# Two steps of the down product moved ahead of a release, and two stores moved ahead of four loads

## What is computed

```python
h = _rmsnorm(x, attn_norm[l])
z = h @ w_in[l]                       # GLA heads and MLA heads
...
x = x + jnp.concatenate([o_gla, o_mla], axis=-1) @ w_out[l]
h = _rmsnorm(x, mlp_norm[l])
x = x + jnp.square(jax.nn.relu(h @ w_up[l])) @ w_down[l]
```

## Time and profile before

| | |
|---|---|
| median of 3 runs | 1158.79 us (1158.64 to 1160.03) |
| the profiled execution's own time | 1160.03 us |
| its span, first to last instruction | 1158.1 us |
| TensorE busy | 1126.1 us, 97% |
| VectorE, GpSimd, ScalarE busy | 786.6, 529.6, 468.7 us |
| mean granted TensorE clock | 0.997 of full speed |
| moved by transfers | 158.42 MB, 137 GB/s |

### The profile page before, as it was taken

The page is one execution under the profiler, slowest core; times in us unless marked ns, Lnnn a source line. Parts: engine busy times, 40 slices in busy tenths (PEclk is TensorE's granted clock), DMA queues, the critical chain, the costliest instruction groups (busy, mean ns, idle before and its releaser), DMA issues.

```text
span 1158.1 us, 15248 instructions
## 1 busy us (share of the span) xinstructions
PE 1126.1 (97%) x5582; PEld 899.3 (78%) x5582; DVE 786.6 (68%) x1092; ACT 468.7 (40%) x891; POOL 529.6 (46%) x429
## 2 busy tenths in 40 slices
PE   5999999999999999999999999999999999999998
PEld 5977677776766768887788888888887888888887
DVE  5575776637777772157488755775798888988863
ACT  5343544315565562056423223322434344344341
POOL 2352442514344363235844444444536565564562
PEclk9998999999999999999999999999999999999999
DMA  7332242372212114323334334331589784466642
GB/s 244 88 110 64 81 149 81 91 224 63 74 33 60 51 38 153 120 92 128 108 112 161 110 127 143 112 109 72 200 288 340 257 296 147 131 188 216 203 120 89
DMA packets 98346, 158.42 MB, mean 137 GB/s; under 512 B 9248, under 2 KB 38960, under 8 KB 98272
## 3 DMA queue, kind: packets, MB, share of 16 engines
q1 hardware_dynamic: 96720, 152.53, 40.0%
q10 hardware_dynamic: 1008, 3.67, 0.9%
q0 software_dynamic: 544, 1.24, 0.6%
HBM read 115.46 MB, written 41.94 MB: 136 GB/s over the span
## 4 chain that ended last, share of the span: by engine, by line
PE 83%; DVE 9%; issue 3%; POOL 2%; ACT 1%; DMA 1%; SPq 0%; ACTq 0%; DVEq 0%; POOLq 0%
PE ps L1808 78%; PE ps L2043 2%; PE ps L1880 1%; DVE g_cum L1375 1%; DVE t_all L1580 1%; DVE t_new L1580 1%; DVE dr_lo L1580 1%; POOL wi_lo L753 1%; DMA gain<-in_attn_norm_dram 1%; DMA up_raw<-in_w_up_dram 1%; PE ps L1823 0%; PE ps L1945 0%; DVE stage L1580 0%; DVE m_qk L1349 0%; DVE m_nm L1525 0%
## 5 line engine op out<-in xcount | busy, mean ns | idle before, releaser
L1808 PE MATMUL ps<-dr_hi,dl_hi 128*128 128x512 f32 x448 | 174.5, 390 | 1.6 <-DVE dr_lo L1580 1.6
L1808 PE MATMUL ps<-dr_hi,dl_lo 128*128 128x512 f32 x448 | 174.3, 389 | 0.0
L1808 PE MATMUL ps<-dr_lo,dl_hi 128*128 128x512 f32 x448 | 174.3, 389 | 0.0
L882 POOL TENSOR_TENSOR ua_lo<-up_raw,ua_hi 128x1024 fp32r<-128x1024 f32 x46 | 116.8, 2541 | 118.3 <-ACT ua_hi L918 118.3
L904 POOL TENSOR_TENSOR dl_lo<-l_raw,dl_hi 128x512 fp32r<-128x512 f32 x64 | 101.5, 1610 | 70.2 <-ACT dl_hi L918 69.8
L1808 PE MATMUL ps<-wi_hi,a_hi 128*128 128x512 f32 (+1 forms) x256 | 105.9, 414 | 5.3 <-POOL wi_lo L753 3.8
L1808 PE MATMUL ps<-a_hi,ua_hi 128*128 128x512 f32 x256 | 99.9, 390 | 2.0 <-ACT u_two L918 1.8
L904 POOL TENSOR_TENSOR dl_lo<-s_all,dl_hi 128x512 fp32r<-128x512 f32 x48 | 75.0, 1582 | 58.4 <-ACT dl_hi L918 57.7
L1808 PEld LDWEIGHTS ps<-dr_hi,dl_hi 128*128 128x128 f32 x448 | 84.1, 188 | 20.3 <-issue 2.8
L1808 PE MATMUL ps<-a_lo,ua_hi 128*128 128x512 f32 x256 | 99.6, 389 | 0.0
L1808 PE MATMUL ps<-a_hi,ua_lo 128*128 128x512 f32 x256 | 99.6, 389 | 0.0
(11 more groups left out here) (218 smaller groups left out, 2422.9 us busy)
## 6 DMA issues: line engine op xcount, KB each, us to landing
r_raw<-in_w_down_dram SPq DMA_DIRECT2D x144, 256.0 KB, 3.4
hidden<-stage SPq DMA_DIRECT2D x72, 256.0 KB, 2.1
up_raw<-in_w_up_dram SPq DMA_DIRECT2D x16, 1024.0 KB, 5.5
l_raw<-hidden SPq DMA_DIRECT2D x64, 256.0 KB, 3.3
raw<-in_w_in_dram SPq DMA_DIRECT2D x24, 256.0 KB, 3.0
z_gla<-z_stage SPq DMA_DIRECT2D x16, 256.0 KB, 2.0
raw<-in_w_out_dram SPq DMA_DIRECT2D x16, 256.0 KB, 6.7
xs<-in_x_dram SPq DMA_DIRECT2D x8, 512.0 KB, 7.2
```

Source lines behind the costliest of these rows:

```text
L882: pool.tensor_tensor(ua_lo[n % UP_RING][:, :, :], up_source(g, product), ua_hi[n % UP_RING][:, :, :].bitcast(F32), ALU.subtract).then_inc( ...
L1808: return pe.matmul(dst, lhsT, rhs, start=start, stop=stop, skip_group_check=onto)
```

## The change

In `up_group` for the last group, all four steps 0 to 3 of the down product are prepared ahead of the `u_three` additions; before, steps 0 and 1 were ahead of them and 2 and 3 behind. On SP, the stores of tiles 5 and 7 of the last group go ahead of loads 8 and 9, and the other three stores (8, 9, 6) ahead of loads 10 and 11; before, loads 8 to 11 were all issued ahead of these five stores. Nothing else changes.

```diff
--- before.py
+++ after.py
@@ -693,13 +693,13 @@
             sp.wait_ge(ulo_done, turn_of(UG - 1, P3) + 1)
             for t in range(2, 8):
                 down_load(t)
-            hidden_stores(UG - 1, (3, 4, 2))
-            for t in range(8, 12):
+            hidden_stores(UG - 1, (3, 4, 2, 5, 7))
+            for t in range(8, 10):
                 down_load(t)
-            hidden_stores(UG - 1, (5, 7, 8, 9, 6))
+            hidden_stores(UG - 1, (8, 9, 6))
 
             sp.wait_ge(ulo_done, UP_PRODUCTS)
-            for t in range(12, PAIRS):
+            for t in range(10, PAIRS):
                 down_load(t)
 
             sp.wait_ge(part_ready, 2 * UP_PRODUCTS)
@@ -1702,7 +1702,7 @@
                     dve.wait_ge(p1_out, 2 * g + i + 1)
                     tt(u, made(g, P6, i), u, ALU.add).then_inc(u2_ready, 1)
                 if g + 1 == UG:
-                    down_steps(0, 2)
+                    down_steps(0, 4)
                 for i in range(2):
                     dve.wait_ge(u2_ready, 2 * g + i + 1)
                     if g >= 1:
@@ -1710,8 +1710,6 @@
                     tt(u_three[:, i, :], made(g, P7, i), u_two[:, g % 2, i, :], ALU.add).then_inc(u3_ready, 1)
                 if g + 1 < UG:
                     up_sums_one(g + 1)
-                else:
-                    down_steps(2, 4)
                 if g == 0:
 
                     dve.wait_ge(x2_stored[NB // 2 - 1], 32)
```

## The result

| | before | after |
|---|---|---|
| median of 6 runs | 1158.86 us | 1169.18 us |
| lowest to highest | 1156.43 to 1160.54 | 1165.86 to 1170.42 |
| profiled execution, its span | 1160.03, 1158.1 | 1166.39, 1164.5 |
| mean granted clock of that execution | 0.997 | 0.996 |

The ratio is 1.0081, 95% interval 1.0064 to 1.0097: slower by 10.3 us or 0.9% on the medians, and above the range's 1167.5. The changed kernel run a second time gave 1168.52 against 1158.34 us, ratio 1.0091 (1.0076 to 1.0106). The forecast was 5.0 us.

A forecast was written before the change was run, and what follows sets the result against it. TensorE, busy 97% of the span, was taken as the bound, waiting 2.3 us for VectorE. Waits of 2.4 + 4.9 = 7.3 us against 2.3 add 5.0 to the median 1158.79: 1163.8 us, range 1160.2 to 1167.5.

The forecast's parts named there:

- Part 1: VectorE, steps 2 and 3 ahead of `u_three`: first `u_three` at 844.65, so P4 waits 2.4 us, bounds none to 4.3.
- Part 2, the issue: SP's queue: load 8 is issued at 861.9, 13 us later than before, behind stores 5 and 7 waiting for data.
- supply, 5.0 us: Loads 8 to 12 at 0.75 us per transfer make quad 2 wait: 5.0 us more TensorE waiting in all, chance 62%.
- low 11: End of `down_low(11)` on VectorE, which quad 2's fourth step needs: forecast 878.7 against 873.70 before.
- 0.6 + 0.6 us: VectorE's `down_sum(12)` and then `down_low(11)` after load 12's last transfer, 0.6 us each.
- upper bound of 8.0: Supply loss if each transfer takes 0.93 us: `down_low(11)` ends at 881.7, +8.0 us.
- 1.63 us of waiting between 870 and 874 at full clock: Trace evidence against a clock fall: TensorE with that waiting and 9 matmuls stayed at clock 1.00.
- the fall at 94 to 96 us: Trace evidence on the clock: granted clock goes from 1.00 to 0.50 where 4 matmuls start in 2 us.
- P4's wait alone counts: Rival: supply is quick enough, quad 2's fourth step only +0.1 us, 1158.9; 16% together with late supply under 2.3 us.
- The other side: Rival: early steps 2 and 3 at 0.6 us per operation remove quad 2's wait, giving back 2.3 us, 1156.5; chance 5%.
- The clock falls: Rival: TensorE's clock halves for some 6 us around 872 to 879, costing 3 us more, 1166.8; chance 15%.
- The catching up of steps 12 to 15: After quad 2, step 15 is not late: the ring gives it back with 0.9 us to spare, no later pause.

The follow-up runs named there:

- filled kernel: Changed kernel plus matmuls whose results nobody reads in TensorE's waits before P4 and before steps 9, 10 and 11 of quad 2: 1166.18 us, ratio 1.0071.
- queue's half: Kernel before with only SP's new order of stores and loads, VectorE's order unchanged: 1168.16 us, ratio 1.0092.
- VectorE's half with filled waits: Kernel before with only steps 2 and 3 ahead of `u_three`, plus 10 unread matmuls ahead of P4's wait: 1159.43 us, ratio 1.0009.
- VectorE's half: Kernel before with only steps 2 and 3 ahead of `u_three`, SP's queue unchanged: 1161.72 us, ratio 1.0031.

## Why the prediction was right and where it was wrong

The direction was right, and so was the mechanism of the supply. Two terms of the sum failed: supply was mis-sized, and the fall of the clock, which the sum had at nothing, took place.

*Part 1* held nearly to the number. `u_three` starts at 842.91 and its first half is done at 843.5, 844.5 on the scale of the earlier trace rows, where 844.65 was worked out; P4 waits 2.3 us (2.4). The turns with GpSimd are as in the trace before: sums and lows at 1.7 us until 841.5. By the Trainium skill (SBUF — State Buffer, Who interferes with whom) a VectorE instruction with two SBUF inputs contends with a GpSimd one that reads SBUF, the second to start is blocked until the first is done, and one with a single SBUF input is not; the trace agrees: `t_all` and `dr_lo` 1.7 us, `u_three` with its PSUM input 0.64.

*Part 2, the issue.* Load 8 at 860.57, on the scale before 861.6; 861.9 predicted.

*Part 2, the term that was mis-sized: supply, 5.0 us.* Two pieces of it were too small. One is the rate. The first transfer lands at 863.3, 864.3 on the scale before (864.7 worked out), load 12's last at 877.4: 17 transfers in 14.2 us, 0.83 each in place of 0.75. On the scale before low 11 ends at 879.7 and not at 878.7, 6.0 us late. In the second profile it is 6.6 late, in the filled kernel 7.0, though the transfers there take 0.85 and 0.81 us each. The other piece is the 0.6 + 0.6 us for `down_sum(12)` and `down_low(11)` behind load 12, which left GpSimd out. In the filled kernel load 12's last transfer lands at 876.5, and low 11 ends 2.7 us behind it, as VectorE takes turns with two `dl_lo` of GpSimd:

```profile
875.01 3.09 POOL L904 TENSOR_TENSOR dl_lo<-s_all,dl_hi 128x512 fp32r<-128x512 f32 x2 [1.81 <-ACT dl_hi L918]
...
875.16 1.79 DVE L1580 TENSOR_TENSOR dr_lo<-t_all,dr_hi 128x512 fp32r<-128x512 f32 x1
876.88 1.77 DVE L1580 TENSOR_TENSOR t_all<-r_raw 128x512 f32<-128x512 f32 x1
878.58 0.68 DVE L1580 TENSOR_TENSOR dr_lo<-t_all,dr_hi 128x512 fp32r<-128x512 f32 x1
```

In the queue's half the tail is 2.7 us too, in the two profiles of the changed kernel 1.3 and 1.6. The price of 1.7 us beside GpSimd was in the prediction, but was not used here. In the timed executions supply costs 7.5 to 7.8 us (filled kernel), near the upper bound of 8.0; but that bound stood for 0.93 us each, and in the changed kernel, the filled one and the queue's half the transfers take 0.81 to 0.85. The 0.93 was itself misread: the 5.2 us of the earlier trace rows are the median of load 3's two `w_down` transfers (4.5 and 5.9), so the last one lands at 838.4 and not at 837.7, which makes 1.07 us each.

*The term that was left out: the clock.* The sum had it at nothing, and gave its fall a chance of 15%. It fell in each of the two profiles of the changed kernel, behind both waits; the granted clock is near 0.5, the lower level of 1.2 GHz, for about 4 us. Behind P4 it is absorbed by quad 2's wait; behind quad 2 it is not, and the last matmul is 1.3 us later than low 11 alone would have it. Changed less filled is 1168.5 - 1166.2 = 2.3 us on the medians. For the price I had 3. What I held against it, 1.63 us of waiting between 870 and 874 at full clock, is no argument for waits of 2.3 us in one piece. Nor was the fall at 94 to 96 us, which I read as that of a TensorE that mostly waits: TensorE is recorded as busy for the whole 2.00 us there, with the thin products of the last section. The rule named ahead (the Trainium skill, TensorE: Matmul & The Clock Gate, What's actually happening), that activity releases the throttle, spoke against the change; the trace agrees, as the clock of 0.52 to 0.63 behind a wait of 2.3 us shows.

On the medians the 5.0 became 7.8 with the waits filled and 2.3 more without, which make up the 10.2 by the way they are taken. In the profiled execution the same two are 6.0 and 1.3, together 7.3. It is one of the faster of its kind (1166.39 us, where they reach from 1164.19 to 1170.79), and the 2 to 3 us between the two sums are in no kept profile.

*The rivals.* "P4's wait alone counts": the payback is real, as VectorE's half with filled waits shows (+0.7 us), but supply decides. "The other side": it needed sums and lows at 0.6 us; they took 1.7 beside GpSimd, and `u_three` ended late. "The clock falls": it should have been the likeliest case, and its 1166.8 was too low by the supply's error. The catching up of steps 12 to 15 held; there is no later wait.

Not settled: why timed executions of the changed kernel mostly have a lower clock (0.993, 0.994) than its profiled one (0.996), whether a longer stretch or one more. Its 25 executions lie in groups about 1.9 us apart (1166.4, 1168.3 and 1170.2 us), near the 1.8 of the kernel before, so part of this is the early fall; but only one of them has 0.997 or more, where 19 of 59 of the kernel before have 1.000. Nor is it settled what sets the rate of a burst between 0.66 and 1.07 us for a transfer.

## What to carry to other kernels

In a queue that issues in order, a store that waits for its data holds back every load behind it; the loads whose slots were free cost nothing here as long as they were issued first. Where the matrix engine is nearly always busy, count a wait at more than its length: behind the waits of 2.3 us in these kernels the clock fell, which cost 1.7 us and more for each, even where the wait itself was made up. When a burst sets the time, price what stands behind its last transfer too, with the engine that contends for it: here 1.3 to 2.7 us and not 1.2.

## What was not expected of the hardware

Unread matmuls in a wait make the kernel faster, by keeping the granted clock at 1.00: 2.7 us in VectorE's half, where no two executions overlap, and 2.3 in the changed kernel, where they do. And four thin products, 16 rows deep, with TensorE recorded as busy, let the clock fall to 0.50 at about 96 us in some executions; the kernel's own spread of up to 5 us goes with the mean clock, 1156.4 to 1158.2 us at 1.000 and 1159.9 to 1161.6 at 0.997.
